# Levels of the inverses and chunk steps of the first recurrence, each run whole instead of interleaved

## The chip, the cores and the metric

One core of one Trainium2 chip. The metric is the device time of one launch in microseconds, median of the runs. Engines: TensorE (PE, its weight loads PEld), VectorE (DVE), ScalarE (ACT), GpSimd (POOL), SyncE (SP, which here only starts transfers).

## The reference, cut to what matters

Two transformer-like blocks run one behind the other on 1024 tokens of 1024 features. The first mixes tokens with an RWKV-7 recurrence over 8 heads of 64 beside a causal convolution, then has a convolutional feed-forward part; the second has another recurrence. Only the first recurrence is touched:

```python
def step(S, inp):
    r_t, w_t, k_t, v_t, a_t, b_t = inp
    sa = jnp.einsum("bhvk,bhk->bhv", S, a_t)
    S = S * w_t[:, :, None, :] + sa[..., None] * b_t[:, :, None, :] + v_t[..., None] * k_t[:, :, None, :]
    y = jnp.einsum("bhvk,bhk->bhv", S, r_t)
    return S, y
```

## The kernel before

**Stages.** The program is a row of scopes, each with its own block of five instruction streams: norm, input projections, the first recurrence (`recurrence1`), the convolution's norm, output projection, feed-forward, and the same again for the second block. Between scopes the engines meet. The recurrence's data is all in SBUF; its only transfers are a few constants at its start.

**Chunks.** Tokens are cut into 16 chunks of 64 and these into 4 quarters of 4 chunks. A quarter is worked on as 16 blocks of 64x64 for each of two heads (4 pairs of heads times 4 chunks; the two heads of a pair lie on partitions 0 to 63 and 64 to 127). Two halves `b` of 8 blocks share most operations.

**The inverses.** Inside a chunk, each token's removal term depends on those before it, which calls for the inverse of a triangular 64x64 matrix per block. It is built by doubling, in levels 1 to 5. A level has, for each half: 16 products T of the masked scores with the inverse so far (`level_t`, products at L1136, two records for each), ScalarE's copy of them out of PSUM (`level_out`, L746), 16 products X (`level_x`, L1147), VectorE's sum into `xx` (`level_sum`, L909) and its transpose into `xt` (`level_turn`, L914). X waits for the copy and for the transpose of the level before; T of the next level waits for the sum. GpSimd makes the masked scores of level l into one of two buffers (`mask_level`, L666): from level 3 on, level l's mask waits for T of level l - 2.

**The chain.** The state goes through the 16 chunks in order. Step c of a quarter: products with the keys (`chain_g_keys`, L1167, issued at the end of the step before) and with the state (`chain_g_state`, L1178), ScalarE's copy `gs` (`chain_g`, L750); products that need neither (`chain_between`, L1191, L1196, L1198); products of the inverse with `gs` (`chain_u` on TensorE, L1207) and VectorE's copy `us` (`chain_u` on VectorE, L926); then products with `us` (`chain_s` on TensorE: L1215 for the state, L1222 for the output), and VectorE's sum and decay of the state (`chain_s` on VectorE, L935 and L940).

**The order.** Each engine takes its instructions in the order in which they are written, and it waits on semaphores for the others. The loop over quarters i, on each engine, puts the levels of quarter i beside the chain of quarter i - 1. Chunk step 0 goes before the levels, steps 1 to 3 go into levels 1 to 3, piece by piece between the pieces of the two halves. On TensorE the order within a level is T of half 0, state products of the chain, T of half 1, between products, X of half 0, U, X of half 1, S with output and next keys. VectorE has sum of half 0, `us`, transpose of half 0, sum of half 1, the state's two operations, transpose of half 1. ScalarE has copy of half 0, `gs`, copy of half 1. Quarter 0 has levels and no chain; after the loop the chain of the last quarter runs with no levels. Work for the next quarter stands behind level 1 (VectorE: the scan, L866; TensorE: `key_spread`, L1096) and behind level 2 (VectorE: `key_norm`, L853, and `key`, L870; ScalarE: the exponentials, L733 and L734). Behind level 3 ScalarE copies the results of the chain (L765). All semaphores count up, so a wait names how many of its kind must be done, whatever is put between.

Of the kernel before, what the change touches and what calls it, by code (L numbers as in the profile page):

```python
# [540 lines left out]
def recurrence1(nc, ins, consts, table, ident, rkv, low):  # L541
# [10 lines left out]
    with Scope(nc, "rec1") as s:  # L552
# [63 lines left out]
        def blocks(b):  # L616
            return slice(8 * b, 8 * b + 8)
# [7 lines left out]
        def by_chunk(t):  # L625
            return t.rearrange("p (m n) -> p m n", n=C1)
# [59 lines left out]
        def _(act):  # L686
# [57 lines left out]
            def level_out(l, b, q):  # L744
                act.wait_ge(t_ready, 10 * q + 2 * (l - 1) + b + 1)
                activation(tt[:, blocks(b), :], by_chunk(lv[:, b, :]), ACT.Copy).then_inc(tt_ready, 1)  # L746

            def chain_g(c, q):
                act.wait_ge(g_ready, 4 * q + c + 1)
                activation(gs[:], gu[:, 0, :].rearrange("p (a n) -> p a n", n=N), ACT.Copy).then_inc(gs_ready, 1)  # L750
# [49 lines left out]
            for i in range(QUARTERS):  # L800
                more, back = i + 1 < QUARTERS, i > 0
                if back:
                    chain_g(0, i - 1)
                if more:
                    squares(i + 1)
                    sigmoids(i + 1)
                    key_scale(i + 1)
                    key_std(i + 1)
                for l in range(1, LEVELS):
                    level_out(l, 0, i)  # L810
                    if back and l <= 3:
                        chain_g(l, i - 1)
                    level_out(l, 1, i)
                    if more and l == 2:
                        decays(i + 1)
                    if back and l == 3:
                        results_out(i - 1, more)
                    if back and l == 4:
                        variances(i - 1)
                turns_out(i, (("vt", vt), ("bt", bt)))  # L820
                if back:
                    result_std(i - 1)
                turns_out(i, (("kt", kt),))
                if back:
                    gains(i - 1)
                if more:
                    scores_out(i + 1)
# [8 lines left out]
        def _(dve):  # L836
# [31 lines left out]
            def key(q):  # L868
                dve.wait_ge(kat_ready, q + 1)
                vec.tensor_tensor(by_pair(kf[:]), rows_of(1, q), by_pair(kf[:]), ALU.mult).then_inc(kf_ready, 1)  # L870
# [36 lines left out]
            def level_sum(l, b, q):  # L907
                dve.wait_ge(x_ready, 10 * q + 2 * (l - 1) + b + 1)
                vec.tensor_tensor(xx[:, blocks(b), :], by_chunk(lv[:, b, :]), xx[:, blocks(b), :], ALU.add).then_inc(  # L909
                    xx_ready, 1)  # L910

            def level_turn(l, b, q):
                dve.wait_ge(xx_ready, 10 * q + 2 * l + b + 1)
                vec.transpose(xt[:, blocks(b), :], xx[:, blocks(b), :]).then_inc(xt_ready, 1)  # L914
# [90 lines left out]
            for i in range(QUARTERS):  # L1005
                more, back = i + 1 < QUARTERS, i > 0
                if back:
                    chain_u(0, i - 1)
                first_level(0, i)
                if back:  # L1010
                    chain_s(0, i - 1)
                first_level(1, i)
                if more:
                    key_inverse(i + 1)
                for l in range(1, LEVELS - 1):
                    level_sum(l, 0, i)
                    if back and l <= 3:
                        chain_u(l, i - 1)
                    level_turn(l, 0, i)
                    level_sum(l, 1, i)  # L1020
                    if back and l <= 3:
                        chain_s(l, i - 1)
                    level_turn(l, 1, i)
                    if more and l == 1:
                        scan(i + 1)
                    if more and l == 2:
                        key_norm(i + 1)
                        key(i + 1)
                if more:
                    decayed(i + 1)  # L1030
                for b in range(2):
                    receptance_scores(b, i)
                    last_level(b, i)
                if more:
                    removal(i + 1)
                key_scores(0, i)
                if more:
                    undecayed_key(i + 1)
                for n in range(1, 4):
                    key_scores(n, i)  # L1040
                if back:
                    result_inverse(i - 1)
                for h in range(2):
                    bonus(h, i)
                if back:
                    for h in range(2):
                        normed(h, i - 1)
                    for h in range(2):
                        with_bonus(h, i - 1)
                    for h in range(2):  # L1050
                        gated(h, i - 1)
# [12 lines left out]
        def _(pe):  # L1064
# [64 lines left out]
            def level_t(l, b, q):  # L1129
                pe.wait_ge(lm_ready, 12 * q + 2 * l + b + 1)  # L1130
                pe.wait_ge(xx_ready, 10 * q + 2 * (l - 1) + b + 1)
                if l == 1 and q:
                    pe.wait_ge(xtf_ready, 2 * (q - 1) + b + 1)
                for i in range(8):
                    for hd in heads:
                        last = mm(lv[hd, b, i * C1:(i + 1) * C1], lm[hd, l % 2, 8 * b + i, :], xx[hd, 8 * b + i, :],  # L1136
                                  start=True, stop=True, skip_group_check=True)
                last.then_inc(t_ready, 1)
# [127 lines left out]
            for i in range(QUARTERS):  # L1266
                more, back = i + 1 < QUARTERS, i > 0
                if back:
                    chain_g_keys(0, i - 1)
                    chain_g_state(0, i - 1)  # L1270
                if more:
                    low_rank("decay", 0, i + 1)
                    low_rank("iclr", 0, i + 1)
                if back:
                    chain_between(0, i - 1)
                    chain_u(0, i - 1)
                if more:
                    low_rank("decay", 1, i + 1)
                    low_rank("iclr", 1, i + 1)
                if back:  # L1280
                    chain_s(0, i - 1)
                if more:
                    key_sum(i + 1)
                for l in range(1, 4):
                    level_t(l, 0, i)
                    if back:
                        chain_g_state(l, i - 1)
                    level_t(l, 1, i)
                    if back:
                        chain_between(l, i - 1)  # L1290
                    level_x(l, 0, i)
                    if back:
                        chain_u(l, i - 1)
                    level_x(l, 1, i)
                    if back:
                        chain_s(l, i - 1)
                    if more and l == 1:
                        key_spread(i + 1)
                level_t(4, 0, i)
                level_t(4, 1, i)  # L1300
                if back:
                    centre(0, i - 1)
                level_x(4, 0, i)
                if back:
                    centre(1, i - 1)
                level_x(4, 1, i)
                level_t(5, 0, i)
                level_t(5, 1, i)
                for b in range(2):
                    scores(f"lbr{b}", range(8 * b, 8 * b + 8), 0, i, slice(1, 2))  # L1310
                    level_x(5, b, i)
                pe.wait_ge(bk_ready, 2 * i + 2)
                for n, (name, b) in enumerate((("vt", 0), ("vt", 1), ("bt", 0), ("bt", 1))):
                    scores(f"lk{n}", range(4 * n, 4 * n + 4), 1, i, slice(0, 2))
                    turn(name, b, 2 if name == "vt" else 0, i)
                if back:
                    variance(i - 1)
                for b in range(2):
                    turn("kt", b, 1, i)
                for h in range(2):  # L1320
                    bonus(h, i)
                if back:
                    result_spread(i - 1)
                    for h in range(2):
                        low_rank("gate", h, i - 1)
                if more:
                    for b in range(2):
                        removal_scores(b, i + 1)
# [1304 lines left out]
```

## Time and profile before

| | |
|---|---|
| median of 3 runs | 3818.65 us (3816.97 to 3820.3) |
| the profiled execution | 3817.67 us, its span 3815.9 us |
| PE busy | 3247.6 us (85%) |
| DVE busy | 1509.7 us (40%) |
| ACT busy | 924.1 us (24%) |
| POOL busy | 878.2 us (23%) |
| mean granted clock of TensorE | 0.909 |

Times in the rows are microseconds from the first instruction of the profiled execution; the first recurrence lies between about 345 and 637. A busy share says how long an engine had something running, over stages with different limits. Matmuls are pipelined, and the ends of theirs are modelled, so the distance from one start to the next says more than a duration. The granted clock is 1.00 at 2.4 GHz and 0.50 at 1.2 GHz.

### The profile page before, as it was taken

The numbers are of one execution on the slowest core, as the hardware profiler recorded it, in microseconds if no ns is written. First come the engines' busy times: TensorE is split into PE (matmuls) and PEld (weight loads), VectorE is DVE, ScalarE is ACT, GpSimd is POOL, SyncE is SP. The second block draws the span as 40 slices with busy tenths as digits, with TensorE's granted clock in tenths as the row PEclk, the third lists the DMA queues.
The fourth block names the chain that finished last, engine by engine and source line by source line (L and its number), as shares of the span: only waits on it lengthen the run. The fifth ranks groups of instructions, "written<-read, shape, count | busy, mean of one in ns | idle before, by whom it ended". The sixth has DMA issues, their size and how long they took to land. (4 is left out here: it accounts for less than half of the span.)

```text
span 3815.9 us, 52117 instructions
## 1 busy us (share of the span) xinstructions
PE 3247.6 (85%) x21568; PEld 2837.7 (74%) x21568; DVE 1509.7 (40%) x1630; ACT 924.1 (24%) x1186; POOL 878.2 (23%) x408
## 2 busy tenths in 40 slices
PE   4996998768999999948999957666697799999997
PEld 3785887556777777738999946666696588888886
DVE  2896653233333333340002127677551222232324
ACT  2113432322122122132222232333220221212112
POOL 1222230112112112122222126454411021222211
PEclk8998998779999999969999978777898799999998
DMA  2110000311111111023222320101032111111111
GB/s 83 46 41 19 3 3 2 116 50 44 56 44 33 55 43 34 33 100 92 95 94 89 89 78 18 33 17 34 21 114 89 33 61 39 38 55 44 55 33 61
DMA packets 199427, 199.17 MB, mean 52 GB/s; under 512 B 8685, under 2 KB 173893, under 8 KB 199045
## 3 DMA queue, kind: packets, MB, share of 16 engines
q1 hardware_dynamic: 192965, 173.89, 14.2%
q10 hardware_dynamic: 6336, 23.43, 1.7%
q8 instruction: 99, 1.62, 0.2%
q14 instruction: 27, 0.22, 0.0%
HBM read 161.29 MB, written 36.01 MB: 52 GB/s over the span
## 5 line engine op out<-in xcount | busy, mean ns | idle before, releaser
L1607 POOL TENSOR_TENSOR ffn_w_lo<-ffn_raw,ffn_w_hi 128x1024 fp32r<-128x1024 f32 x88 | 211.5, 2413 | 1187.1 <-ACT ffn_w_hi L1667 1187.1
L1637 PE MATMUL ffn_out<-blk_hi,ffn_w_hi 128*128 128x512 f32 (+1 forms) x1584 | 444.3, 371 | 35.9 <-POOL ffn_w_lo L1607 35.9
L1637 PE MATMUL ffn_out<-blk_lo,ffn_w_hi 128*128 128x512 f32 (+1 forms) x1584 | 441.7, 369 | 0.0
L1637 PE MATMUL ffn_out<-blk_hi,ffn_w_lo 128*128 128x512 f32 (+1 forms) x1584 | 441.1, 369 | 0.0
L364 PE MATMUL proj_out<-in_hi,proj_w_hi 128*128 128x348 f32 (+4 forms) x1408 | 335.3, 340 | 24.6 <-POOL proj_w_lo L353 19.0
L1637 PEld LDWEIGHTS ffn_out<-blk_hi,ffn_w_hi 128*128 128x128 f32 x1584 | 291.2, 191 | 79.7 <-POOL ffn_w_lo L1607 20.2
L1651 PE MATMUL ffn_acc<-ffn_d_hi,ffn_hid_hi 128*128 128x512 f32 x704 | 288.3, 410 | 58.9 <-DVE tokens_x L1761 44.2
L364 PE MATMUL proj_out<-in_hi,proj_w_lo 128*128 128x348 f32 (+4 forms) x1408 | 333.4, 338 | 0.0
L364 PE MATMUL proj_out<-in_lo,proj_w_hi 128*128 128x348 f32 (+4 forms) x1408 | 333.1, 338 | 0.0
L1637 PEld LDWEIGHTS ffn_out<-blk_lo,ffn_w_hi 128*128 128x128 f32 x1584 | 290.2, 190 | 43.1
L1637 PEld LDWEIGHTS ffn_out<-blk_hi,ffn_w_lo 128*128 128x128 f32 x1584 | 289.3, 190 | 43.5
L353 POOL TENSOR_TENSOR proj_w_lo<-proj_w_raw,proj_w_hi 128x1024 fp32r<-128x1024 f32 (+1 forms) x66 | 157.5, 2388 | 673.9 <-ACT proj_w_hi L348 673.9
L1667 ACT ACTIVATE ffn_w_hi<-ffn_raw 128x1024 fp32r<-128x1024 f32 x88 | 90.7, 1052 | 813.3 <-PE ffn_out L1637 800.8
L1651 PE MATMUL ffn_acc<-ffn_d_hi,ffn_hid_lo 128*128 128x512 f32 x704 | 284.8, 405 | 0.0
L1651 PE MATMUL ffn_acc<-ffn_d_lo,ffn_hid_hi 128*128 128x512 f32 x704 | 284.1, 404 | 0.0
L364 PEld LDWEIGHTS proj_out<-in_hi,proj_w_hi 128*128 128x128 f32 (+2 forms) x1408 | 242.3, 188 | 42.4 <-POOL proj_w_lo L353 19.5
L1729 DVE SCALAR_TENSOR_TENSOR ffn_y<-ffn_out,top_table,ffn_y 128x1023 f32<-128x1023 f32 x88 | 112.9, 1282 | 381.0 <-ACT ffn_y L1675 375.1
L364 PEld LDWEIGHTS proj_out<-in_lo,proj_w_hi 128*128 128x128 f32 (+2 forms) x1408 | 243.0, 187 | 15.5
L364 PEld LDWEIGHTS proj_out<-in_hi,proj_w_lo 128*128 128x128 f32 (+2 forms) x1408 | 243.0, 188 | 15.3
L1651 PEld LDWEIGHTS ffn_acc<-ffn_d_hi,ffn_hid_hi 128*128 128x128 f32 x704 | 137.2, 195 | 99.2 <-DVE tokens_x L1761 48.4
L488 DVE SCALAR_TENSOR_TENSOR mixed_conv<-in_c,top_table,mixed_conv 128x1024 f32<-128x1024 f32 x120 | 184.8, 1540 | 3.8
L1761 DVE TENSOR_TENSOR tokens_x<-ffn_acc,tokens_x 128x512 f32<-128x512 f32 x176 | 119.8, 690 | 123.8 <-PE ffn_acc L1651 123.8
(315 smaller groups left out, 4902.0 us busy)
## 6 DMA issues: line engine op xcount, KB each, us to landing
proj<-proj_ev ACTq DMA_DIRECT2D x44, 520.0 KB, 2.7
ffn_raw<-ffn_up SPq DMA_DIRECT2D x44, 512.0 KB, 3.9
proj_w_raw<-w_in SPq DMA_DIRECT2D x44, 512.0 KB, 3.9
ffn_raw<-w_up SPq DMA_DIRECT2D x44, 512.0 KB, 3.9
ffn_d_raw<-ffn_down SPq DMA_DIRECT2D x11, 1024.0 KB, 5.9
ffn_d_raw<-w_down SPq DMA_DIRECT2D x11, 1024.0 KB, 5.9
proj_w_raw<-w_in_first SPq DMA_DIRECT2D x20, 512.0 KB, 4.1
branch_gates<-proj SPq DMA_DIRECT2D x16, 520.0 KB, 4.6
```

The lines of the kernel that those rows point to most:

```text
L353: nc.gpsimd.tensor_tensor(self.lo[:, slot, :, 0:m], self.raw[:, slot, :, 0:m], self.hi[:, slot, :, 0:m], ALU.subtract).then_inc(self.lo_re ...
L364: mm = nc.tensor.matmul(out, w[:, slot, k, 0:m], a[:, k, c0:c0 + c], start=k == 0 and part == 0, stop=k == KD - 1 and part == 2)
L488: nc.vector.scalar_tensor_tensor(conv[:, f, :], c[:, f, t:t + T], table[:, column:column + 1], conv[:, f, :], ALU.mult, ALU.add).then_inc( ...
L1607: G.by(nc.gpsimd.tensor_tensor(w_lo[:, i % 2], raw[:, i % 2], w_hi[:, i % 2], ALU.subtract), f"lo{i}")
L1637: mm = nc.tensor.matmul(o, a[:, i % 2, k, :], b[:, k, first:first + n], start=k == 0 and part == 0, stop=k == KD - 1 and part == 2)
L1651: mm = nc.tensor.matmul(acc[:, t % 3, :], a[:, 1 - par, k, i * P:(i + 1) * P], b[:, k, 512 * h:512 * h + 512], start=k == 0 and part == 0, ...
L1667: A.by(nc.scalar.activation(w_hi[:, i % 2], raw[:, i % 2], ACT.Copy), f"hi{i}")
L1729: V.by(vec.scalar_tensor_tensor(y[:, i % 2, back:T], flat[i % 2][:, 0:T - back], column(at, i), y[:, i % 2, back:T], ALU.mult, ALU.add), name)
L1761: V.by(vec.tensor_tensor(dst, acc[:, t % 3, :], dst, ALU.add), f"down{t}")
```

## The change

In levels 1 to 3, wherever a chain step runs beside them, both halves of the level come first and then the whole chain step, on ScalarE, VectorE and TensorE. GpSimd's and SyncE's streams stay as they are, and so do all operations, their sizes and their waits.

```diff
@@ scalar
                 for l in range(1, LEVELS):
                     level_out(l, 0, i)
+                    level_out(l, 1, i)
                     if back and l <= 3:
                         chain_g(l, i - 1)
-                    level_out(l, 1, i)
                     if more and l == 2:
                         decays(i + 1)
@@ vector
                 for l in range(1, LEVELS - 1):
                     level_sum(l, 0, i)
+                    level_turn(l, 0, i)
+                    level_sum(l, 1, i)
+                    level_turn(l, 1, i)
                     if back and l <= 3:
                         chain_u(l, i - 1)
-                    level_turn(l, 0, i)
-                    level_sum(l, 1, i)
-                    if back and l <= 3:
                         chain_s(l, i - 1)
-                    level_turn(l, 1, i)
                     if more and l == 1:
                         scan(i + 1)
@@ tensor
                 for l in range(1, 4):
                     level_t(l, 0, i)
+                    level_t(l, 1, i)
+                    level_x(l, 0, i)
+                    level_x(l, 1, i)
                     if back:
                         chain_g_state(l, i - 1)
-                    level_t(l, 1, i)
-                    if back:
                         chain_between(l, i - 1)
-                    level_x(l, 0, i)
-                    if back:
                         chain_u(l, i - 1)
-                    level_x(l, 1, i)
-                    if back:
                         chain_s(l, i - 1)
                     if more and l == 1:
                         key_spread(i + 1)
```

## Rows read from the trace of the kernel before

**Rows 1.** Stretch; busy us (instructions) of PE, PEld, DVE, ACT, POOL; clock, DMA, GB/s

```profile
417.00:441.50 24.50, 24.50 (x789) 24.31 (x787) 17.25 (x29) 8.98 (x16) 10.93 (x7) 1.00 0.02 4
...
604.00:624.00 20.00, 17.31 (x515) 15.88 (x513) 7.29 (x16) 2.52 (x7) 0.00 (x0) 1.00 0.02 4
```

**Rows 2.** Timeline (start, us, engine, line, out<-in), PE, level 2, last quarter

```profile
560.76 1.15 PE L1136 MATMUL rec_lv<-rec_xx,rec_lm 64*64 64x64 f32 x32
561.69 0.68 PE L1178 MATMUL rec_gu<-rec_st,rec_ar 64*64 64x64 f32 x16
562.16 1.15 PE L1136 MATMUL rec_lv<-rec_xx,rec_lm 64*64 64x64 f32 x32
563.09 0.68 PE L1191 MATMUL rec_sn<-rec_vt,rec_kt 64*64 64x64 f32 x16
564.49 1.15 PE L1147 MATMUL rec_lv<-rec_tt,rec_xt 64*64 64x64 f32 x32
...
568.22 1.15 PE L1136 MATMUL rec_lv<-rec_xx,rec_lm 64*64 64x64 f32 x32
```

**Rows 3.** Timeline, level 2 of quarter 0, with no chain beside it

```profile
369.38 2.08 PE L1136 MATMUL rec_lv<-rec_xx,rec_lm 64*64 64x64 f32 x64
...
370.57 0.60 ACT L746 ACTIVATE rec_tt<-rec_lv 128x512 f32<-128x512 f32 x1 [4.32 <-PE rec_lv L1136]
370.62 3.56 POOL L666 TENSOR_TENSOR rec_lm<-rec_lba,rec_levels 128x512 f32<-128x512 f32 x2 [3.36 <-PE rec_lv L1136]
...
371.29 2.03 PE L1147 MATMUL rec_lv<-rec_tt,rec_xt 64*64 64x64 f32 x64
371.51 0.60 ACT L746 ACTIVATE rec_tt<-rec_lv 128x512 f32<-128x512 f32 x1 [0.34 <-PE rec_lv L1136]
...
372.44 0.69 DVE L909 TENSOR_TENSOR rec_xx<-rec_lv,rec_xx 128x512 f32<-128x512 f32 x1 [0.57 <-PE rec_lv L1147]
...
374.49 0.71 DVE L914 STREAM_TRANSPOSE rec_xt<-rec_xx 128x512 f32<-128x512 f32 x1
```

**Rows 4.** Timeline, a chunk step of the tail, with no levels beside it

```profile
611.63 0.68 PE L1207 MATMUL rec_gu<-rec_gs,rec_xtf 64*64 64x64 f32 x16
612.35 0.42 DVE L926 COPY rec_us<-rec_gu 128x256 f32<-128x256 f32 x1 [2.69 <-PE rec_gu L1207]
...
612.83 0.68 PE L1215 MATMUL rec_sn<-rec_us,rec_bt 64*64 64x64 f32 x16 [0.52 <-DVE rec_us L926]
...
613.34 0.63 PE L1222 MATMUL rec_yp<-rec_lbr,rec_us 64*64 64x64 f32 x16
```

**Rows 5.** Timeline, level 1 of the last quarter

```profile
551.68 1.55 DVE L940 TENSOR_TENSOR rec_st<-rec_grown,rec_pend 128x256 f32<-128x256 f32 x1
...
553.86 0.71 DVE L905 STREAM_TRANSPOSE rec_xx<-rec_xt 128x512 f32<-128x512 f32 x1
...
554.67 1.15 PE L1136 MATMUL rec_lv<-rec_xx,rec_lm 64*64 64x64 f32 x32 [0.71 <-issue]
...
555.86 0.60 ACT L746 ACTIVATE rec_tt<-rec_lv 128x512 f32<-128x512 f32 x1 [1.47 <-PE rec_lv L1136]
```

**Rows 6.** Timeline, VectorE behind level 2 of quarter 2

```profile
505.53 1.61 DVE L853 SCALAR_TENSOR_TENSOR rec_kk<-mixed_rkv,top_table,rec_e 128x256 f32<-128x256 f32 x4
...
507.06 1.22 DVE L870 TENSOR_TENSOR rec_kf<-mixed_rkv,rec_kf 128x1024 f32<-128x1024 f32 x1
```

**Rows 7.** Timeline, TensorE at half clock; then span and mean clock of the core

```profile
483.31 1.06 PE L1222 MATMUL rec_yp<-rec_lbr,rec_us 64*64 64x64 f32 x16
...
484.16 1.06 PE L1167 MATMUL rec_gu<-rec_vt,rec_lk 64*64 64x64 f32 x16
...
653.03 13.81 PE L1375 MATMUL cln_stats<-cln_ones,cln_square 128*128 128x1 f32 x64 [5.80 <-ACT cln_square L1410]
...
668.16 3.79 PE L1380 MATMUL cln_scale<-top_ident,cln_wide 128*128 128x128 f32 x16 [1.32 <-DVE cln_wide L1395]
...
core 0: 3815.9 us, clock 0.909
```

## Prediction

> **What bounds the kernel now.** I first looked for the stretches in which the change acts. The diff reorders three bodies inside the first recurrence only: levels 1 to 3 of each quarter's inverses, interleaved with chunk steps 1 to 3 of the quarter before. Quarter 0 has nothing behind it and the last four steps have no levels beside them, so three quarters of four are touched, nine levels in all. The table of busy time by stretch shows what ends last there [rows 1]: in the touched stretch that it lists, the three levels beside the first quarter's chain, TensorE is busy for all of the 24.5 us, VectorE for 17, ScalarE for 9, GpSimd for 11, and the DMA share is 0.02. So the touched stretch is bound by TensorE, and the other engines have 7 us and more to spare. The second line is the last quarter's chain, which has nothing to interleave with: there TensorE has gaps (17.3 of 20.0 us).
>
> Next the timeline of TensorE for one whole level, the second one of the last quarter [rows 2]. I read starts, since the ends are modelled. A group here is 16 products of 64x64x64; the level products are two groups each (T for both halves, X for both halves), a step of the chain has six (G, two in the between part plus one for the state, U, S, Y, next keys). From 560.76: T0 takes 0.93, G 0.47, T1 0.93, the between part 1.40, then X0 at 564.49. What is left to the next level's T0 at 568.22 is 3.73 = two X at 0.93 and U, S, Y, keys at 0.466. There is no gap of even 0.1 us. The period is 7.46 us, 16 groups of 0.466. That is the reading on which everything rests: **the interleaved order already runs TensorE without a hole, so another order of the same products can only add holes.**
>
> **What the new order does to one level.** Work is neither added nor removed: same products, copies, sums, transposes, semaphores and counts, no DMA moved. SP issues nothing here. GpSimd's queue isn't edited: its masks wait for T, which comes no later within a level than now. What changes is who stands behind whom. I lay out one level from its T0 = 0.
>
> T0 0, T1 0.93. ScalarE takes T0's half 1.2 us after its start and needs 0.60; then X0 starts 0.12 later. Quarter 0 runs exactly this order already, without a chain, and shows it [rows 3]: T0 369.38, copy 370.57, X0 371.29, so X0 at 1.91 rather than 1.87: a hole of 0.04. X1 follows at 2.84 (the second copy there starts 2.13 after T0 and ends at 2.73). G then starts at 3.77, the between part at 4.24, U at 5.64. The copy of G for U starts 0.7 after G and takes 0.38, ready at 4.85, long before U. VectorE: first sum 1.15 after X0, at 3.07; sum, transpose, sum, transpose end 2.75 later (372.44 to 374.49, plus 0.71) [rows 3], at 5.83.
>
> Now the hole. U, VectorE's copy of it, and S are a strict chain: S can't start before the copy. Today X1, two groups long, sits between U and S and covers it. Behind the change nothing does. The price is in the tail of the recurrence, where the same three stand bare [rows 4]: U 611.63, copy 612.35 for 0.42, S 612.83: 1.20 from U to S where the products take 0.47. The hole is 0.73. Y follows S by 0.51 instead of 0.47, another 0.04. VectorE is free at 5.83 and U's copy wants it at 6.36, so the sums now in front of the copy cost nothing; this cover is 0.53 us thick. S at 6.84, Y 7.35, keys 7.82, next T0 at 8.28. **8.28 against 7.46: 0.82 per level.**
>
> The state: VectorE's two operations after S end 1.6 after S, at 8.45, and G of the next level wants it at 8.28 + 3.77, so that is hidden. Next T0 wants the first sum (3.76) and the mask (made a level ahead): both hidden.
>
> **The nine levels one by one.** Levels 1 and 2 of the two middle quarters begin behind key work with a T0 to G of 0.98 rather than 0.93 and last 7.51 (after taking off the key spread behind level 1); in the new order X0 waits for the copy anyway, so that 0.05 is absorbed: 0.77 each, four of them, 3.1. Level 3 of these two: 0.82 each, 1.6. Levels 2 and 3 of the last quarter: 0.82 each, 1.6. Level 1 of the last quarter is different [rows 5]: T1 there waits until 554.67 for the second half of the first level, which VectorE ends at 554.57 after an operation on the state that took 1.55 instead of 0.43. G fits in that wait today for nothing. Whole order puts G behind X1: from T1, X0 0.93, X1 1.91 (the copy of T1 runs 555.86 to 556.46), G 2.84, between 3.31, U 4.71, S 5.91, Y 6.42, keys 6.89, next T0 7.36, where today it is 6.09 (554.67 to 560.76): 1.27. Sum: 3.1 + 1.6 + 1.6 + 1.3 = 7.6, and 0.1 for level 1 of the middle quarters, where VectorE's two small operations on the key norms may run into the first sum: **7.7 us longer.**
>
> **Other edits.** Key norm and key of the next quarter stand behind level 2 on VectorE. Today they take 2.8 us up to 508.28 [rows 6], beginning when the chain's state is done. New: from 8.48, ending at 11.3, and level 3's first sum is wanted at 8.28 + 3.07 = 11.35. They just fit; if the key runs 0.3 longer under GpSimd's masks, it is eaten by the 0.53 of slack. The scan behind level 1 is covered by the key spread on TensorE (1.97). The exponentials on ScalarE start after G's copy (4.9) instead of after T1's, take 3.4 with their table load, and end at 8.3 against the next copy at 9.4: hidden. Behind level 3, T0 of level 4 and ScalarE's copies of the results follow Y at the distances they have now, so levels 4 and 5 and the scores are moved, not changed. I find no wait behind the levels that would swallow the 7.7 us: all engines depend on TensorE's products and there are no transfers running ahead.
>
> **Unknowns, bounded.** (a) GpSimd's masks run from 1.2 to 3.9 in each level; the sums, now at 4.9, move to 3.07, under them. One row has a sum that starts under masks: 372.44, 0.69 long as elsewhere, with the masks at 3.56 for two instead of 2.5 [rows 3]. Zero is one end; the other is that the first sum waits for the masks to end, at 3.9: last transpose 6.65, U's copy 0.3 later, nine times 0.3 = 2.7. I take zero, by that row. The Trainium skill's GPSIMD Engine Reference (section Specifications, its line on SBUF interfaces) says GpSimd contends with VectorE instructions that have two SBUF inputs or run in a two-port mode. The sum reads one input from PSUM, so by that rule too it would stay free and the sum of terms is 7.7; the state's 1.55 us operation, with two SBUF inputs, agrees with it. (b) TensorE's clock when a quarter begins. In one of three starts it fell to 1.2 GHz: 483.31 to 484.16 for a group is 0.85 instead of 0.47 [rows 7], over S, Y, keys and a part of the product behind them some 1.5 us. Where such falls land isn't tied to this order; I take zero with 1.5 up or down.
>
> **How it stands to the clock on the wall.** The profiled execution had a span of 3815.9 and took 3817.67 us; with 7.7 it would take 3825.4. The median of the runs is 3818.65, 1.0 above; I predict against it: 3826.4.
>
> **Rivals.**
> *Clock lost in the holes.* A hole of 0.73 us in each level brings TensorE down to half clock for a level per quarter. Then 16 groups cost 0.85 instead of 0.466, 6.1 us more, three times 18: 26 us slower in all, 3845; once only, 3833. Against it: the tail has a hole of 0.73 in every 4.8 us and was granted the full 2.4 GHz throughout [rows 1]; the new levels have it in every 8.3. The Trainium skill's TensorE: Matmul & The Clock Gate (A second HAM failure mode) warns of just such micro-idling between groups; the tail row does not bear it out. Chance 0.08.
> *VectorE held under the masks*, (a)'s upper end: 7.7 + 2.7 = 10.4, 3829.1. Chance 0.07.
> *Faster: the clock kept up after the recurrence.* The statistics products of the convolution norm ran at half clock from 653.03 for 13.8 us [rows 7]. If the recurrence's shifted end made the clock stay up through them and through the scale products from 668.16, they would take half: 6.9 and 1.9, together 8.8 against 7.7, which gives 3817.6. From the point where over 7.7 us is regained it ends below the time of before; to be faster by more than a measurement can tell, the same would have to happen at later stages too, and the mean granted clock of 0.909 over the whole [rows 7] leaves room for that. Against it: TensorE's idling in the last part of the recurrence, ahead of the fall, is untouched by the change. Chance 0.04.
> *It does nothing*: every product interleaved now is covered elsewhere, so the holes would have to be filled by the next group. They can't, since TensorE takes products in order. Chance 0.02, 3818.7.
>
> **Numbers.** The forecast's own case has 0.79. About 0.2% (7.6 us) is what a measurement of this kernel can tell from no change, and 7.7 lies on that line: this case is split, 0.43 slower by more, 0.36 within. The small unknowns mostly lengthen, so slightly more than half goes above. With the lost clock and the masks slower gets 0.58; within has "does nothing" and a part of the regained clock besides, 0.39; faster the rest of it, 0.03. Range: 7.7 less clock luck of 1.5 and what spread the runs have (3.3 between the lowest and the highest) gives 3821.5; upwards it takes in the masks' 2.7, and one slow level (3833) with the same luck: 3834.
>
> **What would show it.** Right: in the timeline of the new kernel T0 to next T0 of 8.3 us; U to S 1.20 and a wait of S for VectorE's copy nine times more often, 0.5 to 0.7 each; clock 1.00 in the three stretches; the recurrence longer by about 7.7 and every stage behind it as long as now. Wrong: first sum later than 1.2 us after X0 (masks); groups of 0.85 within levels (clock); a level of 7.5 (something fills the hole); or a stage behind the recurrence that changes length by more than 2 us.

## The result and the profile after

The changed kernel takes 3826.06 us (median of 20 runs, 3822.63 to 3829.19) against 3818.24 for the kernel before (20 runs, 3813.37 to 3820.3): 7.8 us more between the medians. The ratio is 1.0022, with a 95% interval of 1.0016 to 1.0028, which is 6.1 to 10.7 us. Forecast were 3826.4 and 7.7 more. The profiled execution has a span of 3827.4 us, 11.5 above that of before; where the difference between 11.5 and 7.8 may lie is taken up in the experiments below. One execution of each of two kernels further below, "scores first" (9878 us) and "tail and scores" (5943 us), is far slower than the ten others and is left out of the medians.

First the level that [rows 2] show, in the changed kernel: the timeline of TensorE, VectorE and GpSimd for level 2 of the last quarter.

```profile
570.61 2.03 PE L1135 MATMUL rec_lv<-rec_xx,rec_lm 64*64 64x64 f32 x64
571.80 2.51 POOL L666 TENSOR_TENSOR rec_lm<-rec_lba,rec_levels 128x512 f32<-128x512 f32 x2 [5.57 <-PE rec_lv L1135]
572.47 2.03 PE L1146 MATMUL rec_lv<-rec_tt,rec_xt 64*64 64x64 f32 x64
573.62 0.69 DVE L909 TENSOR_TENSOR rec_xx<-rec_lv,rec_xx 128x512 f32<-128x512 f32 x1 [2.85 <-PE rec_lv L1146]
574.34 0.63 PE L1177 MATMUL rec_gu<-rec_st,rec_ar 64*64 64x64 f32 x16
...
575.67 0.71 DVE L914 STREAM_TRANSPOSE rec_xt<-rec_xx 128x512 f32<-128x512 f32 x1
576.21 0.68 PE L1206 MATMUL rec_gu<-rec_gs,rec_xtf 64*64 64x64 f32 x16
576.93 0.42 DVE L926 COPY rec_us<-rec_gu 128x256 f32<-128x256 f32 x1 [0.55 <-PE rec_gu L1206]
577.40 0.68 PE L1214 MATMUL rec_sn<-rec_us,rec_bt 64*64 64x64 f32 x16 [0.52 <-DVE rec_us L926]
577.92 0.63 PE L1221 MATMUL rec_yp<-rec_lbr,rec_us 64*64 64x64 f32 x16
578.39 0.63 PE L1166 MATMUL rec_gu<-rec_vt,rec_lk 64*64 64x64 f32 x16
```

T runs from 570.61, X from 572.47, the chain from 574.34, and the next level begins at 578.85: 8.24 us, where it was 7.46. U at 576.21 and S at 577.40 are 1.19 apart, with TensorE waiting for VectorE's copy, just as in the tail [rows 4]. That makes 0.72 of the 0.78 us; 0.05 more is S to Y, 0.52 where a group takes 0.47. VectorE has ended the last transpose at 576.38 and waits 0.55 for U; the first sum starts under the masks and lasts 0.69, as everywhere.

Who waited for whom in levels 1 to 3 of quarter 1 (total us, times, longest); before, the same three levels show no wait of TensorE for `us`:

```profile
PEld rec_sn L1214 <- DVE rec_us L926: 2.0, 3, 0.7
```

Then stretches, with the columns of [rows 1]: the three levels of quarter 1, the tail, and the two stretches from level 4 of a quarter to level 1 of the next.

```profile
417.50:444.00 26.50, 24.95 (x771) 24.33 (x772) 18.85 (x28) 9.23 (x14) 10.80 (x7) 1.00 0.02 4
615.00:636.00 21.00, 18.08 (x518) 16.48 (x517) 7.65 (x16) 3.52 (x8) 0.00 (x0) 1.00 0.02 4
443.96:492.26 48.30, 43.74 (x874) 38.20 (x870) 24.72 (x36) 23.89 (x43) 7.49 (x6) 0.93 0.01 3
518.70:560.09 41.39, 37.40 (x843) 33.54 (x839) 22.68 (x33) 14.42 (x25) 5.12 (x4) 0.96 0.01 3
```

TensorE is now busy 24.95 of 26.50 us at full clock; the tail is as it was. The last two lines hold what I had not counted. The same work in the kernel before:

```profile
441.50:487.38 45.88, 41.31 (x842) 35.91 (x838) 24.67 (x35) 23.05 (x42) 7.48 (x6) 0.96 0.01 3
511.53:551.44 39.91, 35.92 (x844) 32.05 (x840) 23.60 (x35) 14.41 (x25) 5.32 (x5) 1.00 0.01 3
```

From level 4 of quarter 1 at 440.50 to 487.38 it was 46.88 us, now 48.30; the second was 39.91, now 41.39. No instruction was reordered there, but the clock is lower: 0.93 and 0.96 instead of 0.96 and 1.00 (a fall near the start of the next quarter, at 482 before and 487 now, is in the first stretch of both). In the score stretch behind level 5, per two microseconds, first the changed kernel and then the one before:

```profile
457.00:459.00 2.00, 0.83 (x29) 0.70 (x24) 1.97 (x2) 0.60 (x1) 0.00 (x0) 1.00 0.00 0
459.00:461.00 2.00, 1.20 (x12) 1.20 (x14) 1.89 (x3) 0.00 (x0) 0.00 (x0) 0.70 0.00 0
461.00:463.00 2.00, 2.00 (x36) 2.00 (x34) 0.69 (x1) 0.00 (x0) 0.00 (x0) 0.50 0.00 0
```

```profile
456.00:458.00 2.00, 1.60 (x40) 1.61 (x42) 1.94 (x3) 0.00 (x0) 0.00 (x0) 1.00 0.00 0
458.00:460.00 2.00, 2.00 (x60) 2.00 (x56) 0.81 (x2) 0.60 (x1) 0.00 (x0) 1.00 0.04 8
```

In both kernels TensorE idles for 2 us here, waiting for VectorE; only in the changed one does it then go on at 1.2 GHz for a while. The row of before behind that wait:

```profile
456.40 1.09 PE L1117 MATMUL rec_e<-rec_ar,mixed_rkv 64*64 64x128 f32 x16 [1.97 <-DVE rec_lk L952]
```

Such a fall costs 1.45 us (48.30 - 46.88, 41.39 - 39.91).

So the profiled recurrence, from level 1 of quarter 0 to the first product of the next stage, went from 273.77 us (363.52 to 637.29) to 283.91 (364.70 to 648.61): 10.14 more. By levels: +0.73, +0.78, +0.78 in quarter 1; +0.74, +0.77, +0.78 in quarter 2; +1.20, +0.78, +0.78 in quarter 3: 7.34. The two falls: 1.42 and 1.48. What follows the last level 3 is 0.1 shorter. Behind the recurrence the two profiles take 3178.6 and 3178.8 us. In the repeats further below that part takes 3178.8 and 3175.5 us (before) and 3177.8 and 3178.9 (changed): it differs by up to 3.3 us between profiles of one and the same kernel, so whole spans say less of this change than the recurrence does.

### The profile page after: what moved, and what is told of

Read it like the earlier page. It is cut to its first block and busy times, and to the rows that moved or that the text cites. A ratio compares the mean times of both kernels' runs of the same rounds, so it can differ in the third digit from the quotient of the medians.

```text
span 3827.4 us, 52117 instructions
## 1 busy us (share of the span) xinstructions
PE 3255.0 (85%) x21568; PEld 2843.5 (74%) x21568; DVE 1519.2 (40%) x1630; ACT 925.1 (24%) x1186; POOL 877.8 (23%) x408
```

## The experiments

All times are medians, each against runs of the kernel before on the same chip in the same session. "Whole" means in the order of the changed kernel.

| run | time, us | before, us | ratio (95%) |
|---|---|---|---|
| VectorE as before, rest whole | 3827.77 | 3817.5 | 1.0026 (1.0014 to 1.0037) |
| only VectorE whole | 3840.22 | 3817.5 | 1.0059 (1.0046 to 1.0073) |
| X of half 1 behind U | 3818.95 | 3817.5 | 1.0004 (0.9995 to 1.0013) |
| output products behind U | 3823.18 | 3817.5 | 1.0015 (1.0006 to 1.0024) |
| scores first | 3810.76 | 3817.93 | 0.9980 (0.9971 to 0.9990) |
| tail and scores | 3809.04 | 3817.93 | 0.9977 (0.9968 to 0.9986) |
| whole, scores first | 3816.8 | 3817.3 | 1.0001 (0.9992 to 1.0010) |

**Which engine's order costs.** The first run puts VectorE back:

```diff
                     level_sum(l, 0, i)
+                    if back and l <= 3:
+                        chain_u(l, i - 1)
                     level_turn(l, 0, i)
                     level_sum(l, 1, i)
+                    if back and l <= 3:
+                        chain_s(l, i - 1)
                     level_turn(l, 1, i)
-                    if back and l <= 3:
-                        chain_u(l, i - 1)
-                        chain_s(l, i - 1)
```

> TensorE and ScalarE in the whole order, VectorE in the order of before. Theory (the cost is that X of half 1 no longer stands between U and S on TensorE, VectorE's order is indifferent): as the changed kernel, a level of 8.24 to 8.29 us, U to S 1.20, 7.3 us over before. Rival (VectorE's two sums and transposes now ahead of the copy of U hold it up): 0.3 us or more less per level, 3 us or more below the changed kernel.

Its nine levels last 10.36, 8.30, 7.78 (quarter 1), 10.37, 8.29, 7.78 (quarter 2), 10.52, 8.24, 7.78 us (quarter 3), the changed kernel's 10.37, 8.29, 7.78 (twice) and 10.52, 8.24, 7.78. The theory holds for the levels: given this order on TensorE, VectorE's changes nothing in their length. The timed excess is 10.3 us (5.3 to 14.1), and the profiled recurrence is 10.2 longer than before. VectorE's copy of U, and S, stand as in the changed kernel:

```profile
433.80 0.68 PE L1207 MATMUL rec_gu<-rec_gs,rec_xtf 64*64 64x64 f32 x16
434.52 0.42 DVE L926 COPY rec_us<-rec_gu 128x256 f32<-128x256 f32 x1 [2.61 <-PE rec_gu L1207]
435.00 0.68 PE L1215 MATMUL rec_sn<-rec_us,rec_bt 64*64 64x64 f32 x16 [0.52 <-DVE rec_us L926]
```

The second run changes VectorE alone (the vector hunk of the change on the kernel before, nothing else):

> Only VectorE in the whole order, TensorE and ScalarE as before. Theory (a strict chain U, copy, S on a full TensorE): the copy of U now stands behind the sum and transpose of half 1, whose products X come after U, so S waits until 8.16 us after T0 where TensorE is free at 6.06: a hole of 2.1, a level of 9.6, 19 us over before, 11 to 12 over the changed kernel. Rival (the slack of VectorE swallows its order, cost is TensorE's alone): as before, within 2 us.

```profile
431.43 0.68 PE L1206 MATMUL rec_gu<-rec_gs,rec_xtf 64*64 64x64 f32 x16
...
431.90 1.15 PE L1146 MATMUL rec_lv<-rec_tt,rec_xt 64*64 64x64 f32 x32
...
433.08 0.69 DVE L909 TENSOR_TENSOR rec_xx<-rec_lv,rec_xx 128x512 f32<-128x512 f32 x1
433.81 0.71 DVE L914 STREAM_TRANSPOSE rec_xt<-rec_xx 128x512 f32<-128x512 f32 x1
434.44 0.39 DVE L926 COPY rec_us<-rec_gu 128x256 f32<-128x256 f32 x1
434.88 0.68 PE L1214 MATMUL rec_sn<-rec_us,rec_bt 64*64 64x64 f32 x16 [1.84 <-DVE rec_us L926]
```

The copy of U comes 3 us after U, behind a sum that had to wait for X of half 1. The level lasts 9.61 us, as expected. The whole costs 22.7 us where 19 were expected, with 19 inside the interval (17.6 to 27.9); the profiled recurrence is 25.3 longer. Three levels of quarters 2 and 3 show where more than 19 comes from (stretches from T0 to T0, clock third from the right):

```profile
492.29:506.10 13.81, 11.97 (x274) 11.49 (x273) 7.29 (x10) 1.74 (x4) 2.54 (x2) 0.83 0.01 2
506.10:518.25 12.15, 10.31 (x257) 10.17 (x258) 3.76 (x7) 4.87 (x6) 2.55 (x2) 0.77 0.01 3
...
578.59:589.26 10.67, 8.83 (x263) 8.70 (x260) 4.09 (x8) 1.47 (x3) 2.55 (x2) 0.89 0.01 3
```

Here the clock does fall inside levels, twice, each time within 1.1 us behind a wait of TensorE of 1.84 us. In levels with a hole of 0.73 us in 8.3 it never did, in any of the five profiles of kernels that have it. So something like my rival of the lost clock is seen with a hole of 2.1 us in 9.6; that the size of the hole decides is not shown, since falls lie elsewhere in every order tried here (below). Of the two half measures, VectorE's order alone costs most, and TensorE's and ScalarE's without VectorE's cost as much as the whole.

**Is it the missing cover?** X of half 1 goes back between U and S, and VectorE's copy ahead of the second sum; all else stays whole. TensorE's part of the edit:

```diff
                     level_x(l, 0, i)
-                    level_x(l, 1, i)
                     if back:
                         chain_g_state(l, i - 1)
                         chain_between(l, i - 1)
                         chain_u(l, i - 1)
+                    level_x(l, 1, i)
+                    if back:
                         chain_s(l, i - 1)
```

> The changed kernel with one piece put back: X of half 1 between U and S on TensorE, and VectorE's copy of U ahead of the sum of half 1; T, T, X still stand together, ScalarE whole. Theory: the hole is covered, a level of 7.46 to 7.51 us, the time of before within 1 us. Rival (the pieces of the chain standing together, or T and X standing together, cost something of their own): still 3 us or more over before.

Measured: 1.45 us over before, with an interval from 1.9 under to 5.0 over. The profile is sharper. TensorE is full again; a level from T0 425.56 to 433.07 lasts 7.51. Level 3 of quarters 1 and 2, however, lasts 7.51 where before it was 7.00, and level 1 of quarter 3 9.74 against 9.32: together 1.4 us. A fall of the clock at 605, in the tail, makes 1.2 more, so that the profiled recurrence is 2.6 us longer than before. Level 3's 0.5 comes from VectorE:

```profile
434.30 2.51 POOL L666 TENSOR_TENSOR rec_lm<-rec_lba,rec_levels 128x512 f32<-128x512 f32 x2 [4.99 <-PE rec_lv L1136]
434.94 1.15 PE L1147 MATMUL rec_lv<-rec_tt,rec_xt 64*64 64x64 f32 x32
...
435.62 2.27 DVE L870 TENSOR_TENSOR rec_kf<-mixed_rkv,rec_kf 128x1024 f32<-128x1024 f32 x1
...
437.81 0.68 DVE L909 TENSOR_TENSOR rec_xx<-rec_lv,rec_xx 128x512 f32<-128x512 f32 x1
```

The key of the next quarter, 1.22 us in the kernel before [rows 6], takes 2.27 here, and the sum behind it starts 2.9 after X0 instead of 1.2. Both lie beside GpSimd's masks. What differs is which of the two operations started first. The mask that the key of quarter 1 met, in this run, in the kernel before and in the changed kernel:

```profile
435.54 1.27 POOL L666 TENSOR_TENSOR rec_lm<-rec_lba,rec_levels 128x512 f32<-128x512 f32 x1
...
436.13 2.25 POOL L666 TENSOR_TENSOR rec_lm<-rec_lba,rec_levels 128x512 f32<-128x512 f32 x1
...
437.38 1.27 POOL L666 TENSOR_TENSOR rec_lm<-rec_lba,rec_levels 128x512 f32<-128x512 f32 x1 [5.73 <-PE rec_lv L1135]
```

In this run a mask is being made when the key starts at 435.62, and the key ends at 437.89, 1.08 after the mask. In the changed kernel the key starts at 437.83, again inside a mask, and ends at 439.73, again 1.08 after it. Before, the key started at 436.04 between two masks and took 1.22; there the mask behind it took 2.25 instead of 1.27. The covering piece removed the cost of the hole. The rival's 3 us or more lie within the timed interval, but in the profile levels 2 are 7.51 and 7.48 us long, as in the kernel before, so pieces standing together cost next to nothing of their own there.

**Another cover.** The between part is cut in two, and its output products (two groups of three) go behind U.

```diff
                         chain_g_state(l, i - 1)
                         chain_between(l, i - 1)
                         chain_u(l, i - 1)
+                        chain_between_out(l, i - 1)
                         chain_s(l, i - 1)
```

> The changed kernel, with the between part of the chain cut in two in levels 1 to 3: its products for the state stay ahead of U, those for the output go between U and S. Theory: U to S becomes 1.40 with TensorE full, but G to U has one group instead of three as cover and shows a hole of 0.2 (0.7 to ScalarE's start, 0.38 for the copy, 0.06, less 0.93): a level of 7.7, 2 to 2.5 us over before. Rival (the hole is not for lack of cover): a level of 8.2 as in the changed kernel, 7 us over before.

```profile
431.71 0.63 PE L1177 MATMUL rec_gu<-rec_st,rec_ar 64*64 64x64 f32 x16
432.39 0.38 ACT L750 ACTIVATE rec_gs<-rec_gu 128x256 f32<-128x256 f32 x1 [1.74 <-PE rec_gu L1177]
432.83 0.68 PE L1209 MATMUL rec_gu<-rec_gs,rec_xtf 64*64 64x64 f32 x16
...
434.27 0.68 PE L1217 MATMUL rec_sn<-rec_us,rec_bt 64*64 64x64 f32 x16
```

G to U is 1.12 (a hole of 0.19), U to S 1.44 and full. The level lasts 7.74, as worked out. The run costs 5.7 us, not 2 to 2.5, within an interval of 2.3 to 9.2. The profiled recurrence is 6.1 longer. Of this, 5.1 lie in the levels: 2.2 for holes of the size expected (the hole of 0.23 in each and some 0.2 more in the first level 1), 0.66 more in the two level 3 (7.60 for 7.00, the same slow key, 1.90 us), and 2.2 in a level 1 of quarter 3 of 11.52 against 9.32, in which a fall of the clock lies (560). Another 1.4 come from a fall behind level 5 of quarter 2 (41.34 us from level 4 to level 1 where before it was 39.91), and the rest of the recurrence is 0.4 shorter. The mechanism was right; the sum left out VectorE's key beside the masks and the clock.

**Do the falls of the clock belong to the order?** Both kernels once more, unedited, and again in a later session:

> The kernel before, unedited, once more with a profile, to see whether the falls of TensorE's clock between the levels lie where they lay. Theory (they depend on chance, not on the order): levels of 7.46 to 7.52 us to the hundredth as in the first profile, but other falls, of 1.45 us each, at other quarters. Rival (the falls belong to the kernel): again two, at 393 and 482.

> The changed kernel, unedited, once more. Theory: levels of 8.24 to 8.29 us again; the span is 3827.4 less 1.4 to 1.5 for every fall of the clock that isn't there this time (the first profile had four in the recurrence, two of them, at 459 and 534, where the kernel before had none). Rival (the falls at 459 and 534 come from the order): four again at the same places.

> The changed kernel, unedited, a third profile. Theory (the two extra falls belong to the order): falls again behind level 5 of quarters 1 and 2, 48.3 and 41.4 us from level 4 to the next quarter's level 1. Rival (chance): one or both missing, 46.9 or 39.9.

> The kernel before, unedited, a third profile. Theory (the order sets where the clock falls): 46.9 and 39.9 us from level 4 to the next quarter's level 1 again, no fall in the score stretches. Rival (chance): a fall in one of them, 1.45 us more.

| profile | start of quarter 0's level 1 | recurrence from there, us | level 4 to level 1, quarters 1 and 2 |
|---|---|---|---|
| before, three times | 363.52, 362.85, 363.22 | 273.77, 273.84, 273.75 | 46.88, 46.85, 46.87; 39.91 each |
| changed, three times | 364.70, 362.22, 364.51 | 283.91, 284.00, 283.91 | 48.30, 48.26, 48.31; 41.39, 41.38, 41.38 |

For the second profiles I had expected chance, for the third ones the order. In all three profiles of the changed kernel the clock falls behind level 5 of quarters 1 and 2; in all three of the kernel before it doesn't; the starts of the recurrence differ by up to 2.5 us without moving it. So in the profiles the change costs 10.15 us: 7.34 in its levels and 2.9 in two falls outside them, less 0.1 in what follows. The timed difference is 7.8, and 10.15 lies inside its interval; whether the falls are there in every timed run too, a profile can't say.

That the falls are repeatable does not make them a price of TensorE's new order. The run with VectorE put back has the same TensorE order, the same nine levels and the same wait of 1.97 us ahead of the second key scores, and no fall behind level 5 of quarters 1 and 2; its falls are at 414 and, twice as long, at 486. The first two rows are its stretches from level 4 to level 1, the third is the product group behind that wait:

```profile
444.23:492.68 48.45, 43.89 (x874) 37.60 (x871) 25.66 (x38) 23.88 (x43) 7.48 (x6) 0.93 0.01 3
519.12:558.99 39.87, 35.87 (x843) 32.01 (x839) 23.62 (x35) 14.41 (x25) 5.12 (x4) 1.00 0.01 3
...
460.08 1.09 PE L1117 MATMUL rec_e<-rec_ar,mixed_rkv 64*64 64x128 f32 x16 [1.97 <-DVE rec_lk L952]
```

The run with the output products behind U, whose hole is 0.2 us, does have the fall behind level 5 of quarter 2. No two of the nine orders profiled have all their falls in the same places.

**The idle time ahead of the falls.** In the stretch behind level 5 VectorE works two operations for the next quarter's keys before it takes TensorE's first key scores. They are dealt out between the four score copies instead:

```diff
+                key_scores(0, i)
                 if more:
-                    removal(i + 1)
-                key_scores(0, i)
+                    removed(i + 1)
+                key_scores(1, i)
+                if more:
+                    removal(i + 1)
+                key_scores(2, i)
                 if more:
                     undecayed_key(i + 1)
-                for n in range(1, 4):
-                    key_scores(n, i)
+                key_scores(3, i)
```

(`removed` is the first operation of `removal`, `removal` the second.)

> The kernel before, with VectorE's three operations for the next quarter's keys put singly between the four copies of the key scores instead of two of them ahead of the first: nothing is added. Theory (a product group on TensorE waits there for VectorE with nothing to cover it, the same kind of hole): the second key scores on TensorE start 2.0 us earlier, the fourth 1.9, in three quarters: 5.7 us under before, and a fall of the clock less. Rival (the operations moved are on the path themselves, what waits for them is late next): within 2 us of before.

```profile
450.09 1.07 PE L1123 MATMUL rec_e<-rec_ar,mixed_rkv 64*64 64x128 f32 x16
...
451.20 0.69 DVE L954 TENSOR_TENSOR rec_lk<-rec_e,rec_both 128x512 f32<-128x512 f32 x1 [0.18 <-PE rec_e L1123]
...
451.95 1.09 PE L1123 MATMUL rec_e<-rec_ar,mixed_rkv 64*64 64x128 f32 x16
```

The second key scores follow the first by 1.86 us; before it was 3.98 (452.42 to 456.40). The run is 7.2 us faster (3.8 to 11.1), where 5.7 were expected, and its profiled recurrence is 5.5 shorter. The fall less that I expected is not there: its profile has one more than the kernel before, two of them together at 535.

> The changed kernel with VectorE's key operations put between the score copies as in the run of that name. Theory (the falls of the clock at 459 and 534 in the changed kernel, seen in both its profiles, need TensorE's wait of 2 us just ahead of them): no fall in the score stretch behind level 5 of quarters 1 and 2; levels of 8.24 to 8.29 us, 7.3 us over the run with the scores alone, 1.5 over before. Rival (they come from the levels' holes whatever follows): a fall in the same stretches still, and 10 us over the run with the scores alone.

With the whole order the dealt-out scores show no fall behind level 5: 44.72 and 37.74 us from level 4 to level 1 (the first with a fall at 480, at the start of the quarter, like the one at 482 in the kernel before). That was forecast, but it doesn't show that the two falls of the changed kernel need the wait ahead of them. The wait is not enough for a fall: with VectorE put back it is there and the falls are not. Nor is it needed for one: the double fall at 535 in the run with the scores alone, and one at 465 in the last run below, have no wait of TensorE in the 8 us ahead of them. What these runs show is that both falls are gone in two different orders of VectorE's work; what sets their place stays open.

The levels keep their 8.29. The kernel as a whole ends within a microsecond of before, where I had expected 1.5 more; the interval (3.1 under to 3.8 over) holds both. Against the run with the scores alone, each taken against its own runs of before, the timed difference is 6.7 us. The profiled recurrence is 4.5 longer (272.78 against 268.27): the levels are 7.9 longer, but that other run has a double fall at 535 worth 2.6 us (40.31 against 37.74) and a tail 0.7 longer. My 7.3 left out that a fall can be on the other side of a comparison.

**A version that beats both.** To the scores, the lesson of the levels is added where nothing covered U to S from the start, in the tail:

```diff
                 chain_between(c, q)
                 chain_u(c, q)
+                chain_between_out(c, q)
                 chain_s(c, q)
```

(and the same in step 0 of each quarter).

> As the run before, and in the four chunk steps that have no levels beside them, and in step 0 of each quarter, the between part's output products stand behind U. Theory: a tail step of 4.78 us becomes 4.3, since U starts 0.9 us earlier less the 0.2 in which it waits for ScalarE's copy, and U to S is 1.40, covered; four steps give 2.0 us, step 0 of the last quarter 0.5: 2 to 2.5 us under the run with the scores alone, 8 under before. Rival (the state's path through S and VectorE sets the step, not U): as the run with the scores alone.

```profile
603.41 0.68 PE L1184 MATMUL rec_gu<-rec_st,rec_ar 64*64 64x64 f32 x16
...
604.57 0.68 PE L1216 MATMUL rec_gu<-rec_gs,rec_xtf 64*64 64x64 f32 x16
...
606.02 0.68 PE L1224 MATMUL rec_sn<-rec_us,rec_bt 64*64 64x64 f32 x16
...
607.68 0.68 PE L1184 MATMUL rec_gu<-rec_st,rec_ar 64*64 64x64 f32 x16
```

G to G is 4.27 us where it was 4.78, with U to S now full. The run is 8.9 us under before (8 expected) and 1.7 under the scores alone in the medians, with the runs of the two overlapping; the profiled recurrences differ by 2.6. The tail is 2.7 shorter, of which the four steps make 2.0, and the rest cancels. The half microsecond expected of step 0 of the last quarter is not seen: from level 4 to level 1 ahead of it 37.79 us, against 37.74 in the run above, which has step 0 as before. And a fall, twice as long as a single one, lies behind level 5 of quarter 1, though the wait of 2 us is gone there too:

```profile
465.00:472.00 7.00, 6.04 (x88) 5.23 (x88) 2.58 (x4) 2.37 (x5) 1.27 (x1) 0.53 0.01 4
```

## Why the prediction was right, point by point

**TensorE bounds the touched stretch, without a hole.** Right. TensorE alone has no hole before, the holes made by the change cost their own length, and putting X back between U and S closed them. (A chain step has eight groups, not the six that the text says; its own list and the 16 groups of the period have eight.)

**0.82 per level.** 0.77 or 0.78 in levels 2 and 3 (forecast: 0.77 for two of the six, 0.82 for four), 0.73 and 0.74 in level 1 of quarters 1 and 2 (forecast: 0.77). Of the term, the hole of 0.73 and the late Y of 0.04 came as read in the tail. The 0.04 for X0 waiting for the copy did not: behind an unbroken level X follows T by 1.86 (570.61, 572.47), since ScalarE starts 1.14 after T0 there. The 1.91 of [rows 3] belongs to a T0 that starts after a pause.

**Level 1 of the last quarter, 1.27.** 1.20: G did lose the free place in T1's wait. The cause given for that wait is not the only one: in two of the three profiles of the changed kernel the state's operation takes 0.43 us instead of 1.55, since it starts just ahead of a mask, and the next operation with two SBUF inputs is slow in its place (560.67, L903, 1.75 us instead of 0.68), so that T1 still waits, 3.19 us from T0 instead of 3.23. **The sum, 7.7:** 7.34 in the profile.

**Slack of 0.53 on VectorE for the sums, and the key eaten by it.** Right, but by a hair. The key of the next quarter behind level 2 of quarter 1, and the sum behind it, in the changed kernel:

```profile
437.83 1.89 DVE L870 TENSOR_TENSOR rec_kf<-mixed_rkv,rec_kf 128x1024 f32<-128x1024 f32 x1
439.65 0.68 DVE L909 TENSOR_TENSOR rec_xx<-rec_lv,rec_xx 128x512 f32<-128x512 f32 x1
```

I had allowed 1.22 and up to 0.3 more; it was 1.89, 0.67 more, because a mask was being made when the key started. The last transpose ends at 442.39 and U's copy is due at 442.50: 0.1 of slack is left, so that it fitted was partly luck. In two experiments (X of half 1 behind U, and output products behind U) level 3 of quarters 1 and 2 was longer by it. The masks did not slow the sums (0.69 and 0.65 under them), so that rival, at 10.4, is out; what they slow is the operation with two SBUF inputs, which is what the Trainium skill's GPSIMD Engine Reference (Specifications) says, and the trace agrees.

**The clock, taken as zero with 1.5 either way.** This is the term that was mis-sized. The step that failed is "Where such falls land isn't tied to this order": in three profiles of three the changed kernel has two more than the kernel before, 2.9 us, so their places do hang on the order, VectorE's included. The forecast of 7.7 met the timed 7.8, but the profiles say 10.15, so a part of the agreement may be luck; both lie within what 20 runs can tell (6.1 to 10.7). The rival of falls inside the levels is out for this change: in three profiles none lies in a level.

**Nothing behind the levels swallows it.** Right: 3178.6 and 3178.8 us from the end of the recurrence, and between 3175.5 and 3178.9 in the repeats of the two kernels.

## What to carry to other kernels

Where one engine is full, look for strict chains (product, copy on another engine, product) and for what stands between their ends: that piece is the cover. Taking it away costs the time from the first product to the last in the bare chain, less the length of the first product. Such a chain standing bare elsewhere in the same trace gave the price to 0.05 us here. Never put the copy behind an operation that waits for products issued after the copy's own: VectorE's order changed alone did that and cost three times the whole change.

## What the runs showed of the hardware

In each of the two kernels that were profiled three times, TensorE's granted clock fell in the same places of the recurrence every time, though the recurrence began up to 2.5 us earlier or later. In other orders of the same work the falls lay elsewhere, even when only VectorE's order differed. Waits of TensorE of 1.1 to 2.1 us stand next to most of the falls, but a wait of 2 us was followed by a fall to 1.2 GHz in one kernel and not in another, with the same TensorE instructions for 15 us before it, and three falls (535 in the run with the scores first, 465 in the one with tail and scores, 605 in the one with X of half 1 behind U) came with no wait in the 8 us ahead. What sets the place, these runs leave open. A single fall costs 1.45 us.

A VectorE operation with two SBUF inputs (128x1024) took 1.22 us when it started between two of GpSimd's masks, and the mask behind it 2.25 instead of 1.27. When it started while a mask was being made it took 1.53 to 2.27 us, and ended 1.08 us after that mask (to 0.01) in each of 27 cases, whatever was left of the mask. VectorE's sums, with one input in PSUM, took at most 0.69 us whether a mask was being made or not.
